# Second input projection: queries and keys written feature-major and rotated there, eight weight blocks moved ahead of the attention

## The reference, cut to what matters

```python
def apply_rope(t, cos, sin):
    t1, t2 = jnp.split(t, 2, axis=-1)
    return jnp.concatenate([t1 * c - t2 * s, t2 * c + t1 * s], axis=-1)

def second_block(x, p, positions, w_in, ...):
    cos, sin = rope_tables(positions, B_QK_DIM)
    h = x @ w_in[i]
    ua, va, za, qh, kh, vh, zb, ga, gb = jnp.split(h, IN_OFFSETS, axis=-1)
    ...
    q = apply_rope(qh.reshape(bn, s_len, B_HEADS, 2, B_QK_DIM), cos, sin) * (B_QK_DIM ** -0.5)
    k = apply_rope(kh.reshape(bn, s_len, B_HEADS, 2, B_QK_DIM), cos, sin)
    o = diff_attention(q, k, vh.reshape(bn, s_len, B_HEADS, B_V_DIM), lam)
    #   per block of 128 queries: softmax of both maps, a = pr0 - lam * pr1, o = a @ v
    o = rms_norm_2(o, b_subln_g[i]) * (1.0 - lam_init)
    yb = o.reshape(bn, s_len, B_WIDTH) * jax.nn.silu(zb)
    ...
```

## Time and profile before

| | us |
|---|---|
| median of 3 runs | 2541.99 (2539.81 to 2542.74) |
| profiled execution, first to last instruction | 2544.3 |
| PE busy in it | 2425.4 (95%) |
| DVE busy | 1172.9 (46%) |
| ACT busy | 908.8 (36%) |
| POOL busy | 748.5 (29%) |
| stage p5, about | 358 |
| attention, 8 heads, about | 744 |

### The profile page before, as it was taken

One profiled execution on the slowest core, in us unless ns is written; L12 is line 12 of the kernel. 1 busy time (PEld: TensorE's weight loads), 2 busy tenths in 40 slices (PEclk: granted clock), 3 DMA queues, 4 the chain that ended last, 5 costly groups with the idle time before them and its releaser, 6 DMA issues.

```text
span 2544.3 us, 41785 instructions
## 1 busy us (share of the span) xinstructions
PE 2425.4 (95%) x16392; PEld 2128.2 (84%) x16392; DVE 1172.9 (46%) x2536; ACT 908.8 (36%) x1686; POOL 748.5 (29%) x725
## 2 busy tenths in 40 slices
PE   6999989999998798999999999999999999999996
PEld 5778968888787698999999889777899777787795
DVE  3001349999996333140000053454454464577535
ACT  4214554444443233131121233333333343554321
POOL 3112224545543121222213232332332332232123
PEclk9999999999999899999999999999999999999998
DMA  4323343343333422132223233133233225375611
GB/s 184 125 108 133 117 158 133 121 142 112 113 132 124 164 103 99 66 115 96 79 95 112 82 117 108 50 124 112 70 105 108 90 89 187 118 270 193 217 54 67
DMA packets 155118, 305.01 MB, mean 120 GB/s; under 512 B 11456, under 2 KB 79680, under 8 KB 143696
## 3 DMA queue, kind: packets, MB, share of 16 engines
q1 hardware_dynamic: 90704, 214.73, 24.2%
q10 hardware_dynamic: 64256, 88.10, 9.7%
HBM read 203.69 MB, written 99.09 MB: 119 GB/s over the span
## 4 chain that ended last, share of the span: by engine, by line
PE 71%; issue 14%; DVE 8%; DMA 2%; POOL 2%; ACT 2%; POOLq 0%; SPq 0%; DVEq 0%; ACTq 0%
PE bank L393 11%; PE bank L395 10%; PE bank L394 10%; PE bank L404 8%; PE bank L405 7%; PE bank L406 7%; PE bank L2087 3%; PE bank L2067 3%; POOL w_lo L359 1%; PE bank L1384 1%; PE bank L2056 1%; PE bank L676 1%; PE bank L2371 1%; DVE w_lo L359 1%; DVE rec_z L1119 1%
## 5 line engine op out<-in xcount | busy, mean ns | idle before, releaser
L404 PE MATMUL bank<-w_hi,at_hi 128*128 128x256 f32 x2432 | 705.7, 290 | 7.7 <-DVE at_lo L1584 6.8
L405 PE MATMUL bank<-w_lo,at_hi 128*128 128x256 f32 x2432 | 692.6, 285 | 0.0
L406 PE MATMUL bank<-w_hi,at_lo 128*128 128x256 f32 x2432 | 692.5, 285 | 0.0
L393 PE MATMUL bank<-at_hi,w_hi 128*128 128x512 f32 x1472 | 608.8, 414 | 5.9 <-ACT stage L429 5.5
L395 PE MATMUL bank<-at_hi,w_lo 128*128 128x512 f32 x1472 | 578.8, 393 | 0.0
L394 PE MATMUL bank<-at_lo,w_hi 128*128 128x512 f32 x1472 | 577.4, 392 | 0.0
L359 POOL TENSOR_TENSOR w_lo<-w_raw,w_hi 128x2048 fp32r<-128x2048 f32 x69 | 318.2, 4611 | 843.3 <-ACT w_hi L372 843.3
L404 PEld LDWEIGHTS bank<-w_hi,at_hi 128*128 128x128 f32 x2432 | 471.7, 194 | 20.9 <-issue 12.0
L405 PEld LDWEIGHTS bank<-w_lo,at_hi 128*128 128x128 f32 x2432 | 471.0, 194 | 0.8 <-issue 0.2
L406 PEld LDWEIGHTS bank<-w_hi,at_lo 128*128 128x128 f32 x2432 | 470.5, 193 | 0.0
L429 ACT ACTIVATE stage<-bank 128x512 f32<-128x512 f32 x272 | 161.9, 595 | 623.4 <-PE bank L395 320.0
(11 more groups left out here) (256 smaller groups left out, 2958.3 us busy)
## 6 DMA issues: line engine op xcount, KB each, us to landing
w_raw<-in_weights SPq DMA_DIRECT2D x84, 1024.0 KB, 7.0
feat<-stage ACTq DMA_DIRECT2D x152, 256.0 KB, 2.0
tok<-stage ACTq DMA_DIRECT2D x104, 256.0 KB, 2.2
stage<-feat SPq DMA_DIRECT2D x32, 256.0 KB, 3.5
x<-in_x SPq DMA_DIRECT2D x4, 1024.0 KB, 9.6
w_mem<-in_w_mem SPq DMA_DIRECT2D x4, 1024.0 KB, 11.5
logg<-gate_g ACTq DMA_DIRECT2D x8, 512.0 KB, 2.8
rec_b<-logg SPq DMA_DIRECT2D x16, 256.0 KB, 5.2
```

Of the source, the lines that this page charges most:

```text
L393: nc.tensor.matmul(ps_gemm[i % 2], wh, ah, start=(k == 0), stop=False)
L404: nc.tensor.matmul(o, ah, wh, start=(k == 0), stop=False)
L405: nc.tensor.matmul(o, ah, wl, start=False, stop=False)
L406: last = nc.tensor.matmul(o, al, wh, start=False, stop=(k == KT - 1))
```

## The change

Queries and keys become eight F blocks in `feat2`. For a head, SP loads the 128 rows of its queries (`dqx`) and of its keys (`dkx`), now in two buffers each, and next to them the same rows with the halves of 32 swapped (`dqs`, `dks`), in four DMAs of 32 rows each. The rotation is three instructions of 1024 columns per engine and head, with tables of [128, 1024] in which the sign is contained. The 16 transposes of a head, both copies out of PSUM and their semaphores are gone. The scores of a head's first turn are issued by PE before `LAST_SLOT` of the head ahead (`first_scores`).

Eight blocks (`UA`, and `ZA`) leave the attention: `gemm_quarters` (18 F blocks: queries, keys, `ZB`, `UA`, half of `ZA`) and `gemm_before` (the other half of `ZA`, during which the tables are computed and the first head is rotated) run in `p5`. The attention keeps 16 blocks, 2 per head, 32 parts. DVE's loop over heads is written out.

```diff
-UA, ZA, ZB, GA, GB = 0, 1024, 2048, 3072, 4096
+UA, ZA, ZB, GA, GB, QF, KF = (n * D for n in range(7))
...
-        gemm2 = [
-            Segment(8, "T", ACT.Copy, tok2, QH),
-            Segment(4, "T", ACT.Copy, tok2, VH),
+        gemm2 = [Segment(4, "T", ACT.Copy, tok2, VH)]
+        gemm_quarters = [
+            Segment(4, "F", ACT.Copy, feat2, QF),
+            Segment(4, "F", ACT.Copy, feat2, KF),
             Segment(4, "F", ACT.Silu, feat2, ZB),
+            Segment(4, "F", ACT.Copy, feat2, UA),
+            Segment(2, "F", ACT.Copy, feat2, ZA),
         ]
+        gemm_before = [Segment(2, "F", ACT.Copy, feat2, ZA + 2 * CB)]
...
-        SLOT_PARTS = [5] + [2, 0, 2] * LONG + [3, 1, 2] * LONG + [3]
+        SLOT_PARTS = [2] + [2, 0, 1] * LONG + [2, 1, 1] * LONG + [2]
...
             Segment(4, "T", ACT.Copy, tok2, VA),
-            Segment(4, "F", ACT.Copy, feat2, UA),
-            Segment(4, "F", ACT.Copy, feat2, ZA),
             Segment(4, "T", ACT.Copy, tok2, PG),
...
         def p5_sp(sp):
...
+            for segs in (gemm2, gemm_quarters):
+                gemm_sp(sp, segs)
+            sp.wait_ge(tile_done, ALL_QUARTERS + 8)
+            for to, of in ((dposi, I["positions"].partition_broadcast(P)), (dfr, I["freq"]),
...
             queries_load(sp, 0)
-            gemm_sp(sp, gemm2[2:])
+            gemm_sp(sp, gemm_before)
...
         def queries_load(sp, head):
...
+            row = head * P
+            if head >= 2:
+                sp.wait_ge(d_s, (head - 1) * 16 + 1)
+            if head:
+                sp.wait_ge(d_rq, 3 * head)
+                sp.wait_ge(d_rk, 3 * head)
+            for x, swapped, at, done in ((dqx[head % 2], dqs, QF + row, d_in), (dkx[head % 2], dks, KF + row, d_in)):
+                sp.dma_start(x[:], feat2[at:at + P, :]).then_inc(done, 16)
+                for n in range(4):
+                    other = at + (n ^ 1) * 32
+                    sp.dma_start(swapped[n * 32:(n + 1) * 32, :], feat2[other:other + 32, :]).then_inc(done, 16)
...
+        def rope_third(eng, x, swapped, ready, done, head, third):
+
+            to = x[head % 2]
             if third == 0:
...
+                eng.wait_ge(ready, 160 * (head + 1))
+                eng.tensor_tensor(to[:], to[:], dcos[:], ALU.mult).then_inc(done, 1)
             elif third == 1:
...
+                eng.tensor_tensor(swapped[:], swapped[:], dsin[:], ALU.mult).then_inc(done, 1)
             else:
...
+                eng.wait_ge(done, 3 * head + 2)
+                eng.tensor_tensor(to[:], to[:], swapped[:], ALU.add).then_inc(done, 1)
...
         def p5_pool(pool):
...
+            split_low(pool, g // 2 + 1, 0)
             pool.wait_ge(d_taba, 3)
-            rope(pool, dk, dtk, d_rk, 0)
-            low_of(pool, gemm2[2:])
+            rope(pool, dkx, dks, d_in, d_rk, 0)
+            split_low(pool, g // 2 + 1, 1)
...
         def head_act(act, it):
...
-            act.wait_ge(d_tq, it + 1)
-            nc.scalar.activation(dqT[:], ps_a[:].rearrange("p a n -> p (a n)"), ACT.Copy).then_inc(d_eq, 1)
+            attention_exp(act, it, 0)
             slot_results(act, it, FIRST_SLOT)
-            attention_exp(act, it, 0)
...
         def head_pe(pe, it):
-            pe.wait_ge(d_e, it * 16 + 2)
-            for x, ps, done, ready in ((dq, ps_a, d_tq, d_rq), (dk, ps_b, d_tk, d_rk)):
-                pe.wait_ge(ready, it * 6 + 6)
-                for t in range(NT):
-                    last = nc.tensor.transpose(ps[:, t // 4, (t % 4) * P:(t % 4 + 1) * P],
-                                               x[:, t].rearrange("p m a n -> p (m a n)"), ident[:])
-                last.then_inc(done, 1)
             slot_products(pe, it, FIRST_SLOT)
-            pe.wait_ge(d_eq, it + 2)
-            pe.wait_ge(d_ek, it + 2)
-            attention_scores(pe, it, 0)
...
+            if it < B_HEADS - 1:
+                first_scores(pe, it + 1)
             slot_products(pe, it, LAST_SLOT)
```

More of the change, by code:

```diff
@@ L259, in build @@
         step = sem("step")
-        FILLED0, FILLED1, FILLED2, FILLED3 = (2 * KT * n for n in range(1, 5))
+        FILLED0, FILLED1, FILLED2 = (2 * KT * n for n in range(1, 4))
+        FILLED3 = FILLED2 + 2 * KT
         dve_steps = [0]
@@ L1677, in p4_pool @@
             split_low(pool, gemm_out[1][1].first // 2 + 1, 1)
+        Q_AT = gemm_quarters[0].first
+        Q_BLOCKS = [(s, n // 2, n % 2) for s in gemm_quarters for n in range(s.n)]
+        Q_N = len(Q_BLOCKS)
+        assert Q_AT % 2 == 0
+        ALL_QUARTERS = 4 * (Q_AT + Q_N)
         def p5_pe(pe):
@@ L1686, in p5_pe @@
                     whole_tile(pe, s, 0, b, i, (lambda k, h: FILLED2 + h * KT + k) if b == 0 else None)
-            with pe.Fori(1, s.n // 2) as it:
-                for b in range(2):
-                    for i in range(4):
-                        whole_tile(pe, s, it, b, i)
-            gemm_pe(pe, gemm2[1:])
+            for b in range(2):
+                for i in range(4):
+                    whole_tile(pe, s, 1, b, i)
+            gemm_pe(pe, gemm_quarters)
+            gemm_pe(pe, gemm_before)
         d_in, d_in_v = sem("d_in"), sem("d_in_v")
@@ L1951, in p5_act @@
             s = gemm2[0]
+            for n in range(s.n):
+                for i in range(4):
+                    evacuate(act, s, n // 2, n % 2, i)
+                    if n == 0 and i == 0:
+                        normed_high(act, 1)
+                split_high(act, s, n // 2, n % 2)
+            gemm_act(act, gemm_quarters)
+            s = gemm_before[0]
             for b in range(2):
@@ L1954, in p5_act, with rope_tables @@
                     evacuate(act, s, 0, b, i)
-                    if b == 0 and i == 0:
-                        normed_high(act, 1)
                 split_high(act, s, 0, b)
-            with act.Fori(1, s.n // 2) as it:
-                for b in range(2):
-                    for i in range(4):
-                        evacuate(act, s, it, b, i)
-                    split_high(act, s, it, b)
+                if b == 0:
+                    rope_tables(act)
+        def rope_tables(act):
             act.wait_ge(d_tab, 1)
-            for n in range(2):
-                nc.scalar.activation(dcs[:, n], dcs[:, n], ACT.Sin).then_inc(d_taba, 1)
+            for table in (dcos, dsin):
+                nc.scalar.activation(table[:], table[:], ACT.Sin).then_inc(d_taba, 1)
             act.wait_ge(d_tab, 2)
             nc.scalar.activation(dlam[:, 2:4], dlam[:, 0:2], ACT.Exp).then_inc(d_taba, 1)
-            gemm_act(act, gemm2[1:])
         def p8_act(act):
```

113 lines of the change are left out of this document (45 added, 68 removed).

## The result

The changed kernel takes 2626.04 us (median of 4 runs), the kernel before on the same chip 2540.9 us: a ratio of 1.0335, 95% interval 1.0319 to 1.0351. The forecast had the direction and not the size: 2588 was said, and the time lies 11 us above the range, whose top was 2615, and next to rival 5 (2628). The profiled execution has a span of 2621.1 us.

A forecast was written before the change was run, and what follows sets the result against it. PE's own instructions were taken as the bound. Terms −10.2 − 13.4 + 3 + 17 + 24 + 16 + 8 + 2 = +46 us on 2544.3 gave 2591 profiled, 2588 us median; range 2536 to 2615, the forecast's own 2570 to 2615.

The forecast's parts named there:

- rival 5: Whole load burst ahead of the gate and clock down at turn 4 every time, or tables late: 2628 us, chance 0.06.
- plain multiplication and transposes: Queries and keys as F instead of T blocks in p5, −10.2 us; their 16 transposes per head gone, −13.4 us.
- start with its clock: Attention's start: PE idles about 4.5 us for the first probabilities, 3.0 more than before; +3 us, clock +2.
- turn 4 with its clock: ACT's evacuation and split precede its copy: PE waits 1.9 us, turns 5 and 7 0.1 each; +17 us, clock +8.
- values and gate: Each head's first product with the values waits 3.0 us for late loads: +24 us, plus +16 us of clock.
- the rest of the moved blocks: Eight F blocks moved from attention to p5: 21.76 us each there, 21.76 less per head; by itself zero.
- If the two queues share bytes evenly: Head border: ACT's 1.25 MB take as long as 2.5 MB, about 8.3 us; PE waits 3.0 us per head.
- E + 15: 15 us after LAST_SLOT's tile ends: end of the whole 4.75 MB burst at about 350 GB/s, 7 us of wait.
- the case of unequal rows: If the values' 512-byte rows went singly against 4-KB rows, they would land last, at the burst's end.
- The list of what PE might wait for: Ways to be wrong: first product does not wait, or PE waits elsewhere, above all DVE's combination in turns 2 to 4.
- The clock: Half speed for some 4 us after idle time loses 2 us: +16 at the values, +8 turn 4, +2 start.

The follow-up runs named there:

- e5: Changed kernel with next query and key loads held until values and gate land, and POOL's split held until DVE's turn 0 combination: 2548.14 us, ratio 1.0034.
- e8: Changed kernel with the eight blocks kept in attention and next query and key loads held until values and gate land: 2515.61 us, ratio 0.9904.
- e2: Changed kernel with only POOL's split at a head's end held until DVE's combination in turn 0 of the next head: 2623.77 us, ratio 1.034.
- e1: Changed kernel with SP holding the next head's query and key loads (last head: next stage's loads) until values and gate land: 2564.71 us, ratio 1.0099.
- e6: As e5, with PE's parts redistributed so a head's first block ends before the output product of turn 3: 2534.24 us, ratio 0.9974.
- e11: Changed kernel with the values' load reading 4-KB rows of other data, same bytes, outputs computed from other numbers: 2584.32 us, ratio 1.0172.
- e3: Changed kernel with query and key loads issued earlier, behind a head's weight loads and ahead of its store: 2587.35 us, ratio 1.0187.
- e9: Changed kernel with only the eight swapped-row loads of 128 KB held until values and gate land, q and k still at the border: 2581.56 us, ratio 1.0167.
- e10: As e1, with DVE's small single-column product taking its second operand as a per-partition scalar instead of a tensor: 2556.39 us, ratio 1.0064.

## Why the prediction was right in direction and short in size

The forecast was −23.6 (plain multiplication and transposes), +5 (start with its clock), +25 (turn 4 with its clock) and +40 (values and gate with theirs): +46. The medians of the runs split the measured +86 (2626.0 against 2539.8, the 24 runs of the kernel before beside e5 to e8; the first four gave 2540.9) in one order of undoing; in another order the shares would differ, since e2 shows that waits hide behind one another.

| step | forecast | runs |
|---|---|---|
| plain multiplication, transposes | −23.6 | −24.2 (e8 against before) |
| values and gate, with clock | +40 | +61.3 (after against e1) |
| DVE and POOL | 0 | +16.6 (e1 against e5) |
| split in turn 4, with clock | +25 | +13.9 (e5 against e6) |
| the rest of the moved blocks | +5, start | +18.6 (e6 against e8), with the 5.3 of e6's own waits |

Two steps of the prediction failed: the size of the wait for values and gate, and DVE's combination behind POOL's split, which stood at nothing. A smaller one is the rest of the moved blocks, also at nothing; the clock of turn 4 was put too high and took part of the miss back.

**Values and gate: right mechanism, size off.** "If the two queues share bytes evenly … I take this value" was the step that failed. PE waited 5.5 us a head and not 3.0. e11 comes near an even share with equal rows; with the values' 512-byte rows the gate lands at E + 17 (E is 1790.1 at the border shown), later than the E + 15 that the prediction had for the end of the whole burst. That end was worked out at 350 GB/s, where the border shows 285, and where the even share of the same paragraph has 2.5 MB in 8.3 us, 301 GB/s; at that rate the burst ends near E + 17.5. The prediction named the case of unequal rows, and had it only inside rival 5, together with other mishaps, at 0.06. It also took all eight heads as one: in head 7 the loads of the next stage hold the values up (6.8 us), and 13.4 of e1's gain lie there.

**The collision: a missed term.** The border was worked out for PE, ACT and SP and not for DVE and POOL: with the cover gone the combination of turn 0 moves to 4 us behind the border, onto POOL's split, which the change leaves there (1.8 to 2.0 us of PE's time in each of heads 1 to 7). The list of what PE might wait for named DVE's combination, but in turns 2 to 4 and because of the rotation. This term is nothing while the values are late (e2) and 16.6 us once they are not (e5).

**Turn 4: right in place and mechanism** (1.71 us against 1.9). The waits were 12.2 us in all, and with their clock about 19 (13.9 and the 5.3 of e6's own waits) where 25 was said. The turns 5 and 7 gave nothing.

**Start of the attention: right.** PE idles 3.45 us before the first transposes (4.5 said), and from the first scores to the first store e6 takes 77.0 us where e8, less the T block of 23.04 that it has more there, takes 71.6: +5.4 against +5.

**The rest of the moved blocks: forecast at zero.** Between e6 and e8 another 7.9 us lie in the six heads (424.78 against 546.20 − 129.28 = 416.92), where PE is idle for 8.5 us in short waits with 32 parts and for 0.0 with 48. Of the 8.5 us 7.7 are waits for DVE's combination, most of them brought by e6's own shares. About 3.5 us each come behind the last store and ahead of the first scores; their cause stays open. (The four pieces, 20.2 us, are of the two profiled executions; the medians differ by 18.6.)

**The clock: right in kind.** For the same 2712 instructions PE is busy for 433.58 us in the changed kernel and 416.25 in e6, 2.9 us a head against the forecast's 3. That the two agree is luck: the forecast had 3 us of clock for 5.1 us of idle time a head, and PE was idle for 9.3.

**The range** left out rival 5 as a pile of mishaps. It was the plain upper bound of its largest term, and the two ends of that bound (0.9 and 7 us a head) were known. That its 2628 lies next to the measured 2626 is luck as well: it has 56 us of waits for the values where 43.9 came, and nothing for the combination.

## What to carry to other kernels

Work that an engine does between a request and its use is cover, and moving it away is not free: list every chain that starts at that point (loads, another engine's combination, a split), not only the one that was nearest before. Before small loads that are needed soon are issued beside a large burst, let the queue with the burst wait for them: one wait was worth 61 us here and 31 us in e8, part of it at the last border, where the burst is the next stage's. When two waits lie one behind the other, undoing the hidden one shows nothing (e2), so undo them together before dropping a theory.

## What the runs showed of the hardware

- Loads of one moment on two queues: 512 KB in 512-byte rows took 5.4 us with only stores and the gate beside it (e1), 8.1 beside 1 MB in rows of 4 KB or more (e3, e9) and 11.3 beside 2 MB (10.7 in the median of the heads); in 4-KB rows beside the 2 MB 7.8 us in the median (e11). How long after the store the burst starts counts too: in head 7, 5.9 us with the next stage's loads 4.1 us behind the store, 15.0 with them 0.6 us behind it.
- DVE was held for up to 3.4 us by POOL's two-input split both at a tensor_tensor of a single column and at a tensor_scalar of 128 columns, and passed in 0.22 us with a tensor_scalar of one column.
- Idle times of 1.8 to 2.0 us before the first transposes and of 1.7 us in turn 4 left PE at a clock of 0.98 in three of e1's six heads and at 1.00 in the others; shorter by about 0.25 us at the first place (e10), they left it at 1.00 in all six.
